# Norms and operand splits made piece by piece inside the projections, and squares summed beside the residual update

## The chip, the cores and the metric

The kernel runs on one core of a Trainium2 chip. The metric is the device time of one execution in microseconds (us); less is better. The engines are TensorE (PE in the profile, with its weight loads as PEld), VectorE (DVE), ScalarE (ACT), GpSimd (POOL) and SyncE (SP), which here only issues transfers. PEclk is the granted clock of TensorE as a share of its full 2.4 GHz; 0.50 is the lower level of 1.2 GHz.

## The reference

Two transformer blocks on 1024 tokens of width 1024. The first has two layers with 256 context tokens (1280 columns in all): a layer of attention and a layer of gated linear attention (GLA). The second has 16 meta tokens in front (1040 columns), three mixers, gates and a mixture of experts. What matters here is this frame, which comes three times, and the two residual updates between:

```
def rms_norm(x, g):
    y = x * lax.rsqrt(jnp.mean(x * x, axis=-1, keepdims=True) + EPS)
    return y * g
...
for layer in range(2):
    hx = rms_norm(x, norm_g[layer]) * (1.0 + scx) + shx
    hc = rms_norm(ctx, norm_g[layer]) * (1.0 + scc) + shc
    ox, oc = mixer(hx @ w_in, hc @ w_in)
    x = x + gtx * (ox @ w_out[layer])
    ctx = ctx + gtc * (oc @ w_out[layer])
...
u = rms_norm(concat(meta, x), norm1_g)
p = u @ w_in
...
merged = g0 * ya + g1 * yb + g2 * (fox @ w_out_c)
h = h + merged @ w_o
```

The modulation (shift, scale, gate) of layer 0 comes from `silu(c) @ adaln_w[0]`, made at the very start.

## The kernel before

Activations lie transposed: 128 partitions of features by columns of tokens, in 8 chunks `k` of 128 features. The residual `E.X` stays in SBUF. A projection is computed with three products per weight and operand block: each fp32 operand is split in a rounded high part (`hi`, made by ACT) and a rest (`lo`, made by DVE as operand minus `hi`), and TensorE adds `w_hi*hi + w_hi*lo + w_lo*hi`. A **job** is one block of 128 output features: 8 chunks x 3 products x its column tiles, accumulated in one of two PSUM tiles `acc`. Tiles are `TILES1` (512, 512, 256 columns), `XT` (512, 512), `TILES2` (352, 352, 336) or `TILES3` (512, 512). ACT makes `w_hi` (L616) and DVE `w_lo` (L730) of job i+2 when job i is done; weights are loaded by SP in a ring of three.

The program is a chain of phases, each a block that every engine enters together and leaves together. Six phases only prepare operands for the projection that follows, and the projection starts when the whole phase is over:

1. `setup_phase`: loads parameters, then the weights of the first modulation (8 transfers of 1536 KB, half on SP, half on ACT). TensorE multiplies them (L289). GpSimd loads the residual (L243, 5120 KB) once the second of them has landed.
2. `norm_phase`, three times (before the layer-0, the GLA and the second block's projection): ACT squares each chunk (L330), TensorE sums over partitions with a matrix of ones (L369), ACT takes `rstd` with Ln and Exp (L336, L338), DVE makes `u = x * gain * rstd` (L397), ACT makes `hi` (L354, L352), DVE makes `lo` (L385, L383). SP loads the first two weights (L448), which are split by one ACT and one DVE instruction of 2048 columns (L452, L456) after the second tile.
3. `split_phase`, three times (before the two output projections and the gate projection): SP loads pieces of the mixer's result (L982) in a ring, ACT makes `hi` (L993), DVE `lo` (L1000), then the first two weights. Before the second output projection SP also restores the residual from DRAM (L986), and the phase waits for it.

Within `gemm_phase` a job goes over all its tiles for each chunk and product, the loop that the change takes apart:

```
for k in range(nk):
    kb = (j.k0 + k) * P
    for lhs, rhs in ((whi, hi), (whi, lo), (wlo, hi)):
        first, last = k == 0 and lhs is whi and rhs is hi, k == nk - 1 and lhs is wlo
        for t, (off, n) in enumerate(j.tiles):
            mmi = eng.matmul(a[:, t, 0:n], lhs[:, j.w % 2, kb:kb + P],
```

A job's result leaves PSUM by kind: "store" by ACT (L673), "rope" (L687, L688, `roots`, and DVE) with small products on TensorE in the next job (`rope_aux`), "resid" by DVE into `E.X` (L847), "gate" by DVE (L882 to L890). Job i+2 waits until job i has left its PSUM tile.

## Time and profile before

| what | value |
|---|---|
| time, median of 3 runs | 3600.99 us (3600.76 to 3604.33) |
| profiled execution, its own time | 3605.53 us |
| its span | 3603.7 us |
| PE busy | 2956.3 us (82%) |
| DVE busy | 1624.4 us (45%) |
| ACT busy | 1231.2 us (34%) |
| DMA | 452.02 MB, 125 GB/s over the span |

Busy shares are means over phases that differ much. What a preparation phase costs is read from the stretch between the last work of the phase ahead of it and the first product of the projection.

### The profile page before, as it was taken

The numbers are of one execution on the slowest core, as the hardware profiler recorded it, in microseconds if no ns is written. First come the engines' busy times: TensorE is split into PE (matmuls) and PEld (weight loads), VectorE is DVE, ScalarE is ACT, GpSimd is POOL, SyncE is SP. The second block draws the span as 40 slices with busy tenths as digits, with TensorE's granted clock in tenths as the row PEclk, the third lists the DMA queues.
The fourth block names the chain that finished last, engine by engine and source line by source line (L and its number), as shares of the span: only waits on it lengthen the run. The fifth ranks groups of instructions, "written<-read, shape, count | busy, mean of one in ns | idle before, by whom it ended". The sixth has DMA issues, their size and how long they took to land. (4 is left out here: it accounts for less than half of the span.)

```text
span 3603.7 us, 36460 instructions
## 1 busy us (share of the span) xinstructions
PE 2956.3 (82%) x14078; PEld 2306.6 (64%) x14078; DVE 1624.4 (45%) x2616; ACT 1231.2 (34%) x1972; POOL 159.5 (4%) x258
## 2 busy tenths in 40 slices
PE   7799997957775979996894889999897378748883
PEld 2577885636664758883663679988665267637773
DVE  1566335637774130005553235431243453357786
ACT  2444212435553131113432221111143211237776
POOL 0000000100000000000000000000000020020002
PEclk9899998979997979996897989999999699769997
DMA  5223333253303013221214013333332641269996
GB/s 221 88 105 134 135 122 87 72 155 98 81 8 107 18 53 132 85 70 66 79 36 165 23 60 122 114 102 97 95 97 54 251 133 59 90 238 357 371 384 253
DMA packets 144304, 452.02 MB, mean 125 GB/s; under 512 B 18258, under 2 KB 39378, under 8 KB 142836
## 3 DMA queue, kind: packets, MB, share of 16 engines
q1 hardware_dynamic: 100196, 280.78, 23.1%
q0 software_dynamic: 27520, 98.02, 7.9%
q10 hardware_dynamic: 16416, 70.90, 5.4%
q8 instruction: 112, 1.84, 0.2%
q14 instruction: 60, 0.49, 0.0%
HBM read 322.68 MB, written 126.95 MB: 125 GB/s over the span
## 5 line engine op out<-in xcount | busy, mean ns | idle before, releaser
L948 PE MATMUL acc<-act_hi,w_hi 128*128 128x512 f32 (+3 forms) x2512 | 704.5, 378 | 204.0 <-PEq L967 110.2
L948 PE MATMUL acc<-act_lo,w_hi 128*128 128x512 f32 (+3 forms) x2512 | 685.2, 370 | 0.0
L948 PE MATMUL acc<-act_hi,w_lo 128*128 128x512 f32 (+3 forms) x2512 | 683.5, 370 | 0.0
L948 PEld LDWEIGHTS acc<-act_hi,w_hi 128*128 128x128 f32 x2512 | 449.8, 191 | 300.3 <-issue 220.8
L730 DVE TENSOR_TENSOR w_lo<-w_stage,w_hi 128x1024 fp32r<-128x1024 f32 x114 | 139.7, 1225 | 921.8 <-ACT w_hi L616 921.8
L948 PEld LDWEIGHTS acc<-act_lo,w_hi 128*128 128x128 f32 x2512 | 447.1, 191 | 80.2
L948 PEld LDWEIGHTS acc<-act_hi,w_lo 128*128 128x128 f32 x2512 | 445.5, 190 | 78.7
L616 ACT ACTIVATE w_hi<-w_stage 128x1024 fp32r<-128x1024 f32 x114 | 120.9, 1060 | 1073.2 <-PE acc L948 1073.2
L2670 DVE TENSOR_TENSOR expert_lo<-expert_stage,expert_hi 128x1024 fp32r<-128x1024 f32 x186 | 225.9, 1223 | 80.6 <-ACT expert_hi L2613 78.1
L2613 ACT ACTIVATE expert_hi<-expert_stage 128x1024 fp32r<-128x1024 f32 x186 | 195.8, 1058 | 91.7 <-DMA expert_stage<-in_exp_w 46.4
L1722 DVE TENSOR_REDUCE max<-scores 128x1 f32<-128x256 f32 (+6 forms) x256 | 117.2, 484 | 148.9 <-PE scores L1846 148.0
L1886 PE MATMUL outputs<-probs_t,v_ones 128*128 128x512 f32 (+2 forms) x392 | 172.2, 520 | 2.2 <-ACT probs_t L1677 2.2
L1677 ACT ACTIVATE probs_t<-scores_t 128x512 f32<-128x512 f32 (+4 forms) x196 | 100.6, 514 | 135.6 <-PE scores_t L1872 132.9
L1265 DVE TENSOR_REDUCE stats<-scores 128x1 f32<-128x1280 f32 (+1 forms) x80 | 102.0, 1275 | 70.6 <-PE scores L1419 70.4
L1864 PE MATMUL scores_t<-q_stack,k_hi 128*128 128x512 f32 (+4 forms) x196 | 122.8, 627 | 2.5 <-ACT q_rows L1694 2.5
L1221 ACT ACTIVATE probs<-scores,stats 128x1280 f32<-128x1280 f32 (+1 forms) x80 | 92.2, 1153 | 64.3 <-DVE stats L1271 64.1
L1414 PE MATMUL scores<-k_hi,q_stack 128*128 128x512 f32 (+1 forms) x208 | 88.5, 426 | 30.4 <-DMA k_lo<-rope 29.3
L2835 PE MATMUL expert_up<-expert_hi,slots_hi 128*128 128x512 f32 x248 | 101.8, 410 | 6.4 <-DVE slots_lo L2675 6.4
L673 ACT ACTIVATE out_stage<-acc 128x512 f32<-128x512 f32 (+1 forms) x168 | 80.3, 541 | 64.7 <-PE acc L948 64.7
L1842 PE MATMUL scores<-k_hi,q_stack 128*128 128x256 f32 (+6 forms) x256 | 94.8, 373 | 7.2 <-DVE max L1722 5.7
L2837 PE MATMUL expert_up<-expert_hi,slots_lo 128*128 128x512 f32 x248 | 98.8, 398 | 0.0
L2836 PE MATMUL expert_up<-expert_lo,slots_hi 128*128 128x512 f32 x248 | 98.7, 398 | 0.0
(360 smaller groups left out, 4236.8 us busy)
## 6 DMA issues: line engine op xcount, KB each, us to landing
expert_stage<-in_exp_w SPq DMA_DIRECT2D x186, 512.0 KB, 6.5
w_stage<-in_w_in SPq DMA_DIRECT2D x43, 512.0 KB, 4.3
rope<-out_stage ACTq DMA_DIRECT2D x26, 640.0 KB, 3.6
proj<-out_stage ACTq DMA_DIRECT2D x26, 640.0 KB, 5.3
slots_in<-zero SPq DMA_DIRECT2D x1, 15872.0 KB, 42.3
residual<-slots_in POOLq DMA_DIRECT2D x31, 512.0 KB, 7.3
slots_out<-residual POOLq DMA_DIRECT2D x31, 512.0 KB, 6.7
w_stage<-in_ab_w_in SPq DMA_DIRECT2D x26, 512.0 KB, 5.0
```

The source lines that it names most:

```text
L616: eng.activation(whi[:, w % 2, :], stage[:, w % NSTG, :], ACT.Copy).then_inc(w_hi, 1)
L730: eng.tensor_tensor(wlo[:, w % 2, :], stage[:, w % NSTG, :], whi[:, w % 2, :].bitcast(F32), ALU.subtract).then_inc(w_lo, 1)
L948: mmi = eng.matmul(a[:, t, 0:n], lhs[:, j.w % 2, kb:kb + P], rhs[:, c0 + k, off:off + n], start=first, stop=last)
L1265: chain(eng.tensor_reduce(st[:, q % 4, 0:1], S[s_of[q]][:, 0:u.width], AX, ALU.max))
L1677: eng.activation(pT[0:w, q % 3, c0:512], ST[q % 2][0:w, c0:512], ACT.Exp, scale=SCALE).then_inc(exped, 1)
L1722: eng.tensor_reduce(mx[:, n % 2, h, pc:pc + 1], SP[p % 3][:, 0:k1 - k0], AX, ALU.max).then_inc(max_done, 1)
L1864: eng.matmul(s[:, c0:512], kh[:, c, tok:tok + P], qs[:, n % QS, c0:512], start=True, stop=False)
L1886: eng.matmul(O[n % 2][:, c0:512], v1[0:w, u.pair % VS, u.side, tok // P, :], pT[0:w, q % 3, c0:512], start=fox and b == 0, stop=b == len(u ...
L2613: eng.activation(whi[:, n % R, :], stage[:, n % NS, :], ACT.Copy).then_inc(w_hi, 1)
L2670: eng.tensor_tensor(wlo[:, n % R, :], stage[:, n % NS, :], whi[:, n % R, :].bitcast(F32), ALU.subtract).then_inc(w_lo, 1)
L2835: eng.matmul(UP[j % 2][:], uh, wh, start=k == 0, stop=False)
L2837: mm = eng.matmul(UP[j % 2][:], ul, wh, start=False, stop=k == KD - 1)
```

## The change

`norm_phase` and `split_phase` are gone. `gemm_phase` takes a `Feed`: a list of operand pieces (tile, chunk) that ACT and DVE make inside the projection's own block, ahead of their work on jobs, with the two weights split one by one in between. TensorE waits for each piece by number. The first `lead` = 2 jobs are run tile by tile: tile 0 of job 0, tile 0 of job 1, tile 1 of job 0, and so on; from job 2 on all is as before. In the gate projection `lead` is 0. The columns' square sums come from a running tile `E.sums`, kept in `setup_phase` for the first norm and in the two output projections (ACT squares each updated residual chunk, DVE adds it) for the others; one product per tile with the matrix of ones remains. In `setup_phase` the residual is loaded ahead of the modulation's weights, on SP and ACT. The restore of the residual before the second output projection moves to GpSimd, inside the block. In the layer-0 projection the second job is now a "store" job.

```diff
 setup_phase
@@ sync (scalar the same with odd i)
-            eng.wait_ge(loaded, 48)
+            for i in range(0, KD, 2):
+                eng.dma_start(E.X[:, i, X0:X0 + NT1], dram["x0"][:, i, :]).then_inc(x_in[i], 16)
+                eng.dma_start(E.X[:, i, 0:META], dram["meta"][:, i, :]).then_inc(x_in[i], 16)
             for i in range(0, KD, 2):
                 eng.dma_start(tiles[:, i, :], dram["adaln_w0"][i]).then_inc(w_in[i], 16)
@@ scalar
+            for i in range(KD):
+                eng.wait_ge(x_in[i], 32)
+                if i >= 3:
+                    eng.wait_ge(summed, i - 2)
+                eng.activation(E.sums[:] if i == 0 else sq[:, i % 2, :], E.X[:, i, :], ACT.Square).then_inc(sq_ready, 1)
 gemm_phase
@@ sync
+            if feed.src is not None:
+                load_operand(0)
+            for w in range(NW):
+                if w >= NSTG:
+                    eng.wait_ge(w_lo, w - NSTG + 1)
                 eng.dma_start(stage[:, w % NSTG, :], wdram[w]).then_inc(w_in[w % NSTG], 16)
+                if w == 1 and feed.src is not None:
+                    for i in range(1, len(feed.pieces)):
+                        load_operand(i)
@@ gpsimd
+            if restore is not None:
+                for i in range(KD // 2):
+                    eng.dma_start(E.X[:, 2 * i:2 * i + 2, 0:META + T], restore[:, 2 * i:2 * i + 2, :]).then_inc(restored[i], 16)
@@ scalar
+            if feed.norm is not None:
+                mean_root(0)
+            round_w(0)
+            for i, (t, k, _, _) in enumerate(feed.pieces):
+                operand_high(i)
+                if i == 1:
+                    round_w(1)
+                if feed.norm is not None and k == 5 and t + 1 < len(feed.tiles):
+                    mean_root(t + 1)
             for i, j in enumerate(jobs):
+                if sums and i >= 1:
+                    squares(i - 1)
@@ vector
+            if feed.norm is not None:
+                normalized(0)
+                normalized(1)
+            split_w(0)
+            for i in range(len(feed.pieces)):
+                operand_low(i)
+                if feed.norm is not None and i + 2 < len(feed.pieces):
+                    normalized(i + 2)
+                if i == 1:
+                    split_w(1)
+            eng.wait_ge(fed_lo, len(feed.pieces))
@@ tensor
+            for t in range(len(jobs[0].tiles) if lead else 0):
+                for i in range(lead):
+                    if t == 0:
+                        eng.wait_ge(w_lo, jobs[i].w + 1)
+                    products(i, [t])
@@ in products, ahead of each product
+                            if hi is feed.hi and feed.number.get((c0 + k, off), 0) > fed[0]:
+                                fed[0] = feed.number[c0 + k, off]
+                                eng.wait_ge(fed_lo, fed[0])
```

On TensorE, from the setup to the first projection, stood before (the `acc` rows are job 0):

```order
L289 MATMUL mod_rows_p<-adaln_w,silu_cond 2x512 x48
L294 MATMUL mod<-consts,mod_rows 128x2 x24
L215 UNCONDITIONAL_BRANCH
L363 UNCONDITIONAL_BRANCH
L369 MATMUL ss_31<-sq,consts 128x512 x8
L369 MATMUL ss_32<-sq,consts 128x512 x8
L369 MATMUL ss_33<-sq,consts 128x256 x8
L303 UNCONDITIONAL_BRANCH
L913 UNCONDITIONAL_BRANCH
L948 MATMUL acc_43<-act_hi,w_hi 128x512 x2
L948 MATMUL acc_43<-act_hi,w_hi 128x256
```

and stands now, at the same place (`acc_40` is the PSUM tile of job 1, used for the sums first):

```order
L307 MATMUL mod<-consts,mod_rows 128x2 x23
L216 UNCONDITIONAL_BRANCH
L907 UNCONDITIONAL_BRANCH [waits barrier_Pool_Activation_PE_DVE_SP_release]
L950 MATMUL acc_40<-square_sums,consts 128x512 x2
L950 MATMUL acc_40<-square_sums,consts 128x256
L941 MATMUL acc_39<-act_hi,w_hi 128x512 [waits operand_lo_ready_54,w_lo_ready_45]
L941 MATMUL acc_39<-act_lo,w_hi 128x512
L941 MATMUL acc_39<-act_hi,w_lo 128x512
L941 MATMUL acc_39<-act_hi,w_hi 128x512 [waits operand_lo_ready_54]
L941 MATMUL acc_39<-act_lo,w_hi 128x512
```

24 products of the norm became 3, the phase border between norm and projection is gone, and the projection's first products wait for single pieces.

On ACT, in the layer-0 projection, stood before (`acc_44` is job 1; the first row is the last of the roots of job 0, which wait for small products that TensorE makes inside job 1):

```order
L633 ACTIVATE out_stage<-rope_x 128x256 [waits rope_done_70]
L626 DMA rope<-out_stage 128x1280 [waits out_lo_ready_58]
L626 DMA rope<-out_stage 128x1280
L616 ACTIVATE w_hi<-w_stage 128x1024 [waits w_loaded0_45,products_50]
L687 ACTIVATE rope_sq<-acc_44 128x512 [waits products_50,out_lo_ready_58]
```

and stands now (`acc_40` is job 1):

```order
L561 ACTIVATE out_stage<-rope_x 128x512 [waits rope_done_72]
L561 ACTIVATE out_stage<-rope_x 128x256 [waits rope_done_72]
L554 DMA rope<-out_stage 128x1280 [waits out_lo_ready_60]
L554 DMA rope<-out_stage 128x1280
L544 ACTIVATE w_hi<-w_stage 128x1024 [waits w_loaded0_41,products_46]
L647 ACTIVATE out_stage<-acc_40 128x512 [waits products_46] x2
```

The order is the same, but the small products of job 0 now stand inside job 2, so the split of the fourth weight, which job 3 needs, waits for job 2 where it waited for job 1.

On SP, in the second output projection, stood before (with a phase border ahead of the last row):

```order
L982 DMA stage<-mixed 128x512 x6
L448 DMA w_stage<-in_w_out 128x1024 x2
L982 DMA stage<-mixed 128x512 x10
L986 DMA residual<-residual_x 128x8x1040
L571 DMA w_stage<-in_w_out 128x1024 x6
```

and stands now (the pieces' tiles are named `operand`, six of them in turn):

```order
L486 DMA operand_331<-mixed 128x512
L493 DMA w_stage<-in_w_out 128x1024 x2
L486 DMA operand_332<-mixed 128x512
L486 DMA operand_333<-mixed 128x512
L486 DMA operand_334<-mixed 128x512
L486 DMA operand_335<-mixed 128x512
L486 DMA operand_336<-mixed 128x512
```

The first weights stand behind one piece and no longer behind six, and the restore is on GpSimd's queue.

## Rows read from the trace of the kernel before

**Rows 1.** Busy time by stretch: start:end, length, PE, PEld, DVE, ACT, POOL, PEclk, DMA, GB/s

```profile
64.70:117.40 52.70, 24.48 (x49) 10.39 (x49) 30.45 (x49) 33.81 (x57) 0.00 (x0) 0.66 0.06 20
...
1109.90:1134.90 25.00, 0.00 (x0) 0.01 (x1) 15.38 (x17) 13.59 (x17) 0.00 (x0) 0.50 0.70 252
...
1251.90:1304.90 53.00, 26.31 (x48) 10.94 (x49) 30.45 (x49) 33.76 (x56) 0.00 (x0) 0.64 0.05 20
...
1923.60:1954.00 30.40, 0.00 (x0) 0.00 (x0) 13.11 (x17) 11.87 (x17) 0.00 (x0) 0.50 0.86 313
...
2045.40:2087.40 42.00, 18.48 (x49) 10.39 (x49) 25.00 (x49) 27.95 (x57) 0.00 (x0) 0.74 0.07 25
...
2845.90:2865.50 19.60, 0.02 (x1) 0.05 (x1) 7.69 (x9) 6.81 (x9) 0.00 (x0) 0.50 0.50 161
```

**Rows 2.** The same view around the first norm and the first projection's start

```profile
64.70:81.70 17.00, 15.01 (x29) 6.56 (x30) 0.00 (x0) 12.21 (x19) 0.00 (x0) 0.79 0.19 62
...
117.40:122.80 5.40, 5.40 (x15) 4.43 (x16) 0.00 (x0) 1.22 (x1) 0.56 (x1) 0.50 0.80 297
122.80:150.00 27.20, 27.20 (x131) 21.71 (x130) 7.46 (x11) 9.97 (x16) 0.00 (x0) 0.99 0.24 96
```

**Rows 3.** ACT in order of time: the splits of the third and later weights

```profile
152.21 1.06 ACT L616 ACTIVATE w_hi<-w_stage 128x1024 fp32r<-128x1024 f32 x1 [1.62 <-PE acc L948]
...
1165.76 1.06 ACT L616 ACTIVATE w_hi<-w_stage 128x1024 fp32r<-128x1024 f32 x1 [13.02 <-PE acc L948]
1179.84 1.06 ACT L616 ACTIVATE w_hi<-w_stage 128x1024 fp32r<-128x1024 f32 x1 [13.02 <-PE acc L948]
...
1329.77 1.06 ACT L616 ACTIVATE w_hi<-w_stage 128x1024 fp32r<-128x1024 f32 x1 [8.85 <-PE acc L948]
...
1340.65 1.06 ACT L616 ACTIVATE w_hi<-w_stage 128x1024 fp32r<-128x1024 f32 x1 [8.85 <-PE acc L948]
...
1978.63 1.06 ACT L616 ACTIVATE w_hi<-w_stage 128x1024 fp32r<-128x1024 f32 x1 [9.82 <-PE acc L948]
...
2101.42 1.06 ACT L616 ACTIVATE w_hi<-w_stage 128x1024 fp32r<-128x1024 f32 x1 [12.81 <-PE acc L948]
...
2112.84 1.06 ACT L616 ACTIVATE w_hi<-w_stage 128x1024 fp32r<-128x1024 f32 x1 [5.75 <-PE acc L948]
```

**Rows 4.** DVE in order of time: two pieces running in the first and third norm

```profile
85.95 0.75 DVE L397 SCALAR_TENSOR_TENSOR u<-residual,mod_gain,rstd 128x512 f32<-128x512 f32 x1
...
87.28 0.75 DVE L397 SCALAR_TENSOR_TENSOR u<-residual,mod_gain,rstd 128x512 f32<-128x512 f32 x1
...
2061.56 0.58 DVE L397 SCALAR_TENSOR_TENSOR u<-residual,params,rstd 128x352 f32<-128x352 f32 x1
...
2062.49 0.58 DVE L397 SCALAR_TENSOR_TENSOR u<-residual,params,rstd 128x352 f32<-128x352 f32 x1
```

**Rows 5.** Tile view of the operand's rest: ns min/median/max, first and last start

```profile
L385 DVE SCALAR_TENSOR_TENSOR act_lo<-u,mod,act_hi x48: 475/746/753, 85.3 to 1304.1; 128x512 fp32r<-128x512 f32 x32, 128x256 fp32r<-128x256 f32 x16
```

**Rows 6.** The page's costliest groups: the weights' rests

```profile
L730 DVE TENSOR_TENSOR w_lo<-w_stage,w_hi 128x1024 fp32r<-128x1024 f32 x114 | 139.7, 1225 | 921.8 <-ACT w_hi L616 921.8
```

**Rows 7.** Issue to landing: the first norm's two weights (L448), then the restore (L986)

```profile
DMA to landing us min/median/max: 3.6/4.0/4.5
...
DMA to landing us min/median/max: 15.6/15.6/15.6
```

**Rows 8.** Busy time by stretch, inside the first split phase

```profile
1118.00:1121.00 3.00, 0.00 (x0) 0.00 (x0) 1.75 (x3) 0.85 (x2) 0.00 (x0) 0.50 1.02 412
```

**Rows 9.** The setup: TensorE in order of time, and the residual's load

```profile
15.18 44.08 PE L289 MATMUL mod_rows_p<-adaln_w,silu_cond 128*2 128x512 f32 x96 [15.18 <-DMA adaln_w<-in_adaln_w]
...
residual<-in_x POOLq DMA_DIRECT2D x1, 5120.0 KB, 33.9
```

**Rows 10.** The gate projection: first way out of PSUM, and the third weight

```profile
2871.04 1.42 DVE L882 TENSOR_TENSOR residual<-acc,gates 128x512 f32<-128x512 f32 x2 [5.86 <-PE acc L948]
...
2879.32 1.06 ACT L616 ACTIVATE w_hi<-w_stage 128x1024 fp32r<-128x1024 f32 x1 [16.46 <-PE acc L948]
```

More of the change, by code:

```diff
@@ L837, in _ @@
                     split_w(j.w + 2)
+                if sums and i >= 1:
+                    add_squares(i - 1)
                 a = acc[i % 2]
-                if j.kind == "he":
-                    hidden(i, j)
-                    continue
+                if restore is not None and i % 2 == 0:
+                    eng.wait_ge(restored[i // 2], 16)
                 for t, (off, n) in enumerate(j.tiles):
@@ L951, in _ @@
                                 mmi.then_inc(mm, 1)
-                    if k % 2 == 1 and pending:
+                    if i >= lead and k % 2 == 1 and pending:
                         rope_aux(*pending.pop(0))
-                while pending:
-                    rope_aux(*pending.pop(0))
+            if feed.norm is not None:
+                for t, (off, n) in enumerate(feed.tiles):
+                    eng.matmul(acc[1][:, t, 0:n], col(E.con, CONST_AT, "ones"), feed.norm.sums_of(off, n),
+                               start=True, stop=True).then_inc(ss_done, 1)
@@ new lines, in _ @@
+            for t in range(len(jobs[0].tiles) if lead else 0):
[3 more added lines that the diff above has]
+                    products(i, [t])
+            for i, j in enumerate(jobs):
+                if i >= lead:
+                    eng.wait_ge(w_lo, j.w + 1)
+                    if i >= 2:
+                        eng.wait_ge(free[i % 2], free_before[i])
+                    if j.a.merged:
+                        eng.wait_ge(m_lo, 2 * KD)
+                    products(i, range(len(j.tiles)))
+                    while pending:
+                        rope_aux(*pending.pop(0))
@@ L2924, in out_proj @@
                         gate_of=lambda t, f=f: E.mod[:, layer, 32 + 2 * f + (t == 2):32 + 2 * f + (t == 2) + 1])
-                    for f in range(KD)])
+                    for f in range(KD)], feed, restore=restore, sums=True)
         par = lambda name, j=None: col(E.par, PARAM_AT, name, j)
@@ L2955, in qblocks @@
             return [(P * b, P) for b in bl] + ctxb, masks
+        first.close()
         def head(r, a):
@@ L3006, in build @@
             wts = Weights(nc, c, [d["w_in"][f] for f in order])
-            norm_phase(nc, E, lambda k, off, n: E.X[:, k, off:off + n], TILES2, lambda k, t: par("norm1", k),
-                       lambda k, t: None, hi, lo, wts=wts)
+            norm = Norm(lambda k, off, n: E.X[:, k, off:off + n], lambda off, n: E.sums[:, off:off + n],
+                        lambda k, t: par("norm1", k), lambda k, t: None)
+            feed = Feed([(t, k, *tile) for t, tile in enumerate(TILES2) for k in range(KD)], hi, lo, 2, 4, norm=norm, tiles=TILES2)
             jobs = []
```

433 lines of the change are left out of this document (175 added, 258 removed).

## The prediction

> **What bounds the kernel now.** I read the stretches between phases first, since the change removes phase borders. The busy view shows six stretches in which the projection's products stand still while operands are made [rows 1]: 52.7, 25.0, 53.0, 30.4, 42.0 and 19.6 us, 222.7 us together, 6% of the span. In the three split stretches TensorE does nothing; in the norms it only sums squares. Next I read what fills a stretch. The first norm spends 17.0 us before the first `rstd` exists [rows 2], then DVE paces it: a new 512-column piece starts every 1.33 us (85.95 to 87.28) and a 352-column one every 0.93 us [rows 4]. Third, the jobs: ACT splits a weight when a job ends, so the starts of these splits date the jobs. A job takes 14.08 us with three tiles, 10.88 us with two, 11.42 us with 1040 columns [rows 3]. Last the clock: after each stretch the granted clock is 0.50 for about 5.4 us, 15 products, and 0.99 behind [rows 2], so each projection pays some 2.5 us at its start.
>
> **The yardstick.** For each projection I compare the moment at which job 2 can start, counted from the start S of the preparation. Before, it is the end of job 1, read from the splits [rows 3] and the starts of the stretches [rows 1]: 152.2 - 64.7 = 87.5, 1165.8 - 1109.9 = 55.9, 1329.8 - 1251.9 = 77.9, 1978.6 - 1923.6 = 55.0, 2112.8 - 2045.4 = 67.4 us. From job 2 on the programs are the same.
>
> **First and second norm.** The sums are ready when the block starts, so squares and 21 of 24 fp32 products are gone from the path, and three are left beside the load of the first weight, which lands 3.6 us after issue [rows 7]. Then ACT rounds it, 1.06 us [rows 3], DVE splits it, 1.23 us [rows 6], and the first piece's rest takes 0.75 us [rows 5]; with hand-overs the first product starts at S+7.2. Pieces follow at 1.33 us [rows 4], and the second weight's split puts 1.1 us in: piece 15 at 7.2 + 1.1 + 15 x 1.33 = 28.3, and the 8 pieces of 256 columns at some 0.8 us (two operations of 0.475 us [rows 5], less the overlap) at S+34.7. TensorE needs 3 products a piece and job, 0.68 us at full clock (10.88 / 16 pieces [rows 3]). So tile 0 of job 0 follows DVE to S+18.3, tile 0 of job 1 takes 5.4, tile 1 of both ends at S+35, and in the first norm tile 2 of both, 2.7 us each, at S+40.7. ACT is late next: it is done with pieces at 34.5, and at the end of job 0 (S+38) rounds the third weight and takes job 0 out of PSUM, some 4.4 us: job 2 starts at S+42.5. Its rope work adds what it added to job 1 before, 152.2 - 64.7 - 52.7 - 2 x 14.08 - 2.5 = 4.1 us. And the fourth weight's split now stands behind roots that need job 2. Before, the roots and stores ended with job 1; rounding and split behind them, 1.06 + 1.23 us, now hold job 3, while DVE and the stores ahead do no more than before: 2.5 us, unless another job covers it. First norm: 87.5 - (42.5 + 4.1 + 2.5) = 38.4. In the GLA projection the leading jobs have two tiles, but ACT and DVE first finish the context pieces (S+34.7), then the third weight (2.3 us more with hand-over): job 2 at S+37, gain 77.9 - 37 = 40.9. I take 38 and 41.
>
> **Third norm.** Pieces of 0.93 us [rows 4]: the first at S+6.9, the last at 6.9 + 1.1 + 23 x 0.92 = S+29.2. Job 1's last tile behind it is a third of 11.42: S+33.5. Gain 67.4 - 33.5 = 33.9; I take 33.5.
>
> **First output projection.** The first weight now stands behind one piece and no longer behind six, so the first product comes at S+7.6. At 412 GB/s [rows 8] a 256 KB piece takes 0.64 us; with six slots, 4.0 us to a landing [rows 7] and two splits behind it, 0.8. That is near TensorE's own 0.68, which therefore sets the end: 7.6 + 2.5 (low clock) + 28.2 = S+38.3, and the third weight's split and DVE's way out make it S+39. Gain 55.9 - 39 = 17. The third weight's load is issued behind all 23 pieces, about S+22, and needed at S+35, so it is covered. **Second output projection.** GpSimd issues the restore at once. It took 15.6 us alone [rows 7]; beside the pieces both halve the rate, and the first product comes at S+9.3. Sixteen pieces at 1.3 us last to S+27, TensorE needs until 9.3 + 2.5 + 2 x 10.88 = S+33.6, or 35.7 where it waits. Gain 55.0 - 35.7 = 19. Before, the phase waited for this restore; now DVE wants its first quarter only at S+33.
>
> **What is added.** ACT's squares and DVE's additions run inside jobs that last 10.9 or 14.1 us and cost nothing, but not behind the last job: DVE adds 2 or 3 tiles at 0.7 us (1.42 us for two [rows 10]), 3.2 us for both projections. **Gate projection.** Its first two jobs need no pieces and start at S+7, but DVE takes nothing out of PSUM until all 16 pieces are split, at 0.8 us each about S+17, where it did so at 2871.0 - 2845.9 = S+25.2; the third weight was rounded at S+33.4 [rows 10]. Gain 7, bounds 3 and 9.
>
> **Setup.** Here the change costs. TensorE works without a break from 15.2 to 59.3 [rows 9], fed by the first weight, and the residual came after. Now 5120 KB of residual on two queues stand ahead. By the shapes SP moves 0.98 MB of parameters, 2.65 MB of residual and 1.57 MB of weight until then; at half of 412 GB/s [rows 8] that is 25 us, and with 2 us to the first byte TensorE starts at 27: 12 us lost, with nothing to cover it. Bounds: 0, if SP's queue had the whole rate; 15, if the 1024 short rows of meta tokens cost extra. I take 12, as both queues are full from the start. The residual itself took 33.9 us behind the weights [rows 9], which shows that a queue's place decides. The Trainium skill ("DMA: Bandwidth & Descriptors", section "Issuing engines are not separate DMA queues") says that transfers of all issuers run on the same 16 engines and interleave. By that rule the residual delays the weights by its bytes whoever issues it, 12 to 13 us, as in my sum.
>
> **Sum.** 38 + 17 + 41 + 19 + 33.5 + 7 - 3.2 - 12 = 140.3. TensorE is only half busy while it follows the pieces, so some time at low clock is likely behind them: I take off 1 us for each of five projections. 135 us less of the profiled execution's 3605.5, which lies 4.5 above the median of the runs shown; from the median 3601 it gives 3466.
>
> **Rivals.**
> *The low clock stays through both leading jobs* (0.07). While it waits for pieces, TensorE at half clock needs all of the 1.33 us (2 x 0.68), at full clock half. For it: the norm stretches, with TensorE busy 24.5 of 52.7 us, show 0.66, and the following work starts at 0.50 [rows 1, 2]. Against: that busy time is scattered, while at the low level the pieces keep it full, as in the 5.4 us that raised the clock [rows 2]. Price: leading jobs at twice the time, ends at S+59, 59, 48, 50 and 48: 80 us in all; of 140 remain 60, 3541. [...]
> *A piece goes hand to hand* (0.05): `u`, `hi`, `lo` one after the other, 0.75 + 0.72 + 0.75 = 2.2 us in place of 1.33. Against: [rows 4] already show the overlap with one piece ahead, and now two are. Price 19 + 19 + 16 us, 3520.
> *Slower* (0.02): the low clock outlasts the leading jobs. A three-tile job would take 28 and not 14 us. With the first rival's 80 us, 60 are left, so five such jobs decide it; two more in each of five projections, 12 us each in the mean, give 3601 - 60 + 120 = 3661. Against: in [rows 2] the clock rises within 5.4 us of full work.
> *It doesn't do what it says* (0.03): the setup loses 15 and early starts end in ACT's late ways out, each projection half of its gain: 155.5 / 2 - 3.2 - 15 = 60, 3541.
>
> **How the numbers follow.** My forecast has 0.83. Its own range is 3445 to 3495: setup without loss and gate at 9 (-14), clock kept (-5), against setup at 15, 2 to 5 us more in each of five projections. The range to hold it 8 in 10 reaches toward the rivals, all on one side: 3442 to 3510. A measurement tells 0.2%, 7 us: faster 0.97, same 0.01 (a part of the last rival), slower 0.02.
>
> **What would show it.** The first L302 product of the setup at about 27 us and its end at 71; the first L941 product 7 to 9 us after each block starts; job 2 at S+42, 39, 37, 36, 34; granted clock over 0.9 across the leading jobs behind the first 8 pieces; L782 every 1.33 us; the restore landing without a wait. Wrong would be a clock of 0.5 to the end of job 1, pieces over 2 us apart, or a setup that ends at 60.

## The result, and the profile after

The changed kernel takes 3482.49 us (median of four runs), the kernel before 3600.88 us in the same comparison. One of the four (4906.55 us, mean granted clock 0.566) was disturbed: it is left out of the ratio, but not of this median, and the other three have 3475.6, 3478.8 and 3486.17. The ratio is 0.9664, with a 95% interval of 0.9643 to 0.9685, or 121 us less (113 to 129). The forecast was 3466, 135 less. The profiled execution took 3478.8 us with a span of 3476.9, 126.8 less than the span of before.

I cut the span at the first transfer that SP issues in each block, in order of time:

```profile
84.22 0.81 SPq L493 DMA_DIRECT2D w_stage<-in_ab_w_in  x2
...
1087.82 0.32 SPq L486 DMA_DIRECT2D operand<-mixed  x1
...
1214.24 0.80 SPq L493 DMA_DIRECT2D w_stage<-in_gla_w_in  x2
...
1843.65 0.32 SPq L486 DMA_DIRECT2D operand<-mixed  x1
...
1953.14 1.28 SPq L493 DMA_DIRECT2D w_stage<-in_w_in  x3
...
2720.75 0.32 SPq L486 DMA_DIRECT2D residual<-fox  x1
```

Against the starts in [rows 1] this gives the length of each part. The forecast column has the terms of the prediction's sum, the tail of the square sums halved between the output projections:

| from the start of ... to the next | before | after | difference | forecast |
|---|---|---|---|---|
| setup | 64.7 | 84.2 | +19.5 | +12 |
| layer-0 projection, attention | 1045.2 | 1003.6 | -41.6 | -38 |
| first output projection | 142.0 | 126.4 | -15.6 | -15.4 |
| GLA projection and layer | 671.7 | 629.4 | -42.3 | -41 |
| second output projection | 121.8 | 109.5 | -12.3 | -17.4 |
| third norm's projection to branches | 800.5 | 767.6 | -32.9 | -33.5 |
| gate projection to the end | 757.8 | 756.2 | -1.6 | -7 |
| low clock, allowed for | | | | +5 |
| sum | | | -126.8 | -135 |

**Setup.** TensorE in order of time, then the two queues until 37 us and, below, from 10 to 20 us (packets, MB, share of the 16 engines' time; q1 is SP's, q10 ACT's):

```profile
36.73 42.85 PE L302 MATMUL mod_rows_p<-adaln_w,silu_cond 128*2 128x512 f32 x96 [36.73 <-DMA adaln_w<-in_adaln_w]
```

```profile
q10 hardware_dynamic: 1707, 8.88, 58.8%
q1 hardware_dynamic: 1753, 5.51, 38.4%
...
DMA packets 1406, 4.17 MB, mean 417 GB/s; under 512 B 769, under 2 KB 769, under 8 KB 1285
...
q10 hardware_dynamic: 703, 2.74, 67.9%
q1 hardware_dynamic: 703, 1.43, 36.8%
```

The first product comes 21.5 us later than in [rows 9], and since it waits for SP's first weight, SP's share decides. From 10 to 20 us the packets of both queues are equally many (703 and 703), their bytes are not: ACT's are twice as large. The Trainium skill ("DMA: Bandwidth & Descriptors", section "Queues, rings and completion order") says that each DMA engine alternates between queues packet by packet. The trace agrees. It has a packet for each row, and 769 of the 1406 are under 512 B: most of these are the 64-byte rows of the meta tokens, each of which takes a turn of its queue. By the sizes of the packets in the trace they are 346 of SP's 703 packets in these 10 us, and 121 of ACT's 703 are already rows of weights, 12 KB each. From 5 to 10 us, with SP's queue on parameters and long rows and ACT's with 240 of the 64-byte rows, the packets were equal again (438 and 428), and SP's queue had the larger part of the bytes, 1.30 MB against 0.74.

**Leading jobs.** Busy time by stretch, columns as in [rows 1]: the layer-0 projection to job 2, the second output projection (in two stretches), the third norm's projection (in two), the gate projection to job 2:

```profile
84.20:91.10 6.90, 4.04 (x7) 1.76 (x7) 3.38 (x5) 5.83 (x7) 0.00 (x0) 0.75 0.86 320
91.10:110.00 18.90, 16.22 (x59) 11.12 (x60) 18.90 (x29) 11.18 (x17) 0.00 (x0) 0.91 0.23 78
110.00:125.60 15.60, 14.51 (x87) 12.83 (x85) 9.02 (x20) 8.63 (x16) 0.70 (x1) 1.00 0.22 71
1851.40:1869.20 17.80, 14.23 (x28) 8.11 (x29) 8.97 (x13) 8.51 (x13) 0.00 (x0) 0.50 1.00 385
1869.20:1884.80 15.60, 15.60 (x69) 12.89 (x69) 4.94 (x7) 4.23 (x6) 0.00 (x0) 1.00 0.44 155
1959.50:1970.00 10.50, 9.70 (x35) 8.33 (x36) 10.44 (x22) 5.79 (x12) 0.00 (x0) 0.58 0.33 101
1970.00:1986.00 16.00, 16.00 (x103) 16.00 (x102) 12.63 (x27) 8.89 (x19) 0.00 (x0) 1.00 0.00 1
2720.20:2742.00 21.80, 8.44 (x25) 6.42 (x25) 10.23 (x21) 8.23 (x18) 1.67 (x3) 0.66 0.69 213
```

In the norms DVE is the full column while pieces run; the clock is up after a few us in the layer-0 projection and within 10.5 us in the third. In the layer-0 and the GLA projection it rose behind six products back to back, and then stayed at 1.00 through groups of three products every 1.33 us. In the second output projection the clock stays at 0.50 for 17.8 us, with the wires full (385 GB/s). In the gate projection TensorE is busy 8.4 of 21.8 us. Pieces in the first norm's projection, DVE in order of time, answer to [rows 4]: 1.33 us apart.

```profile
101.34 0.75 DVE L782 SCALAR_TENSOR_TENSOR rope_t<-residual,mod_gain,square_sums 128x512 f32<-128x512 f32 x1
102.67 0.75 DVE L782 SCALAR_TENSOR_TENSOR rope_sq<-residual,mod_gain,square_sums 128x512 f32<-128x512 f32 x1
```

TensorE in order of time, where jobs 2 and 3 start in the layer-0 projection, and job 2 in the first output, the GLA, the second output, the third norm's and the gate projection:

```profile
125.64 0.70 PE L941 MATMUL acc<-act_hi,w_hi 128*128 128x512 f32 x2 [1.13 <-ACT rope_x L664]
...
146.19 0.70 PE L941 MATMUL acc<-act_hi,w_hi 128*128 128x512 f32 x2 [2.43 <-DVE w_lo L696]
...
1126.23 0.70 PE L941 MATMUL acc<-act_hi,w_hi 128*128 128x512 f32 x2 [1.40 <-DVE residual L840]
...
1249.83 0.50 PE L941 MATMUL acc<-act_hi,w_hi 128*128 128x512 f32 x1 [1.00 <-DVE w_lo L696]
...
1884.82 0.61 PE L941 MATMUL acc<-act_hi,w_hi 128*128 128x512 f32 x2
...
1987.32 0.64 PE L941 MATMUL acc<-act_hi,w_hi 128*128 128x352 f32 x3
...
2741.95 1.19 PE L941 MATMUL acc<-act_hi,w_hi 128*128 128x512 f32 x2 [6.33 <-issue]
```

Minus the starts, job 2 of the first five: 41.4, 38.4, 35.6, 41.2 and 34.2 us (forecast 42.5, 39, 37, 35.7 and 33.5); job 3 of the first waits 2.43 us (forecast 2.5). On the page, the idle time ahead of the products' first group fell from 204.0 us, most of it at phase borders, to 119.1:

```profile
L941 PE MATMUL acc<-act_hi,w_hi 128*128 128x512 f32 (+3 forms) x2512 | 730.3, 380 | 119.1 <-DVE act_lo L792 44.6
```

### The profile page after: what moved, and what is told of

Same layout as the page of the kernel before. It is cut to its first block and busy times, and to the rows that moved or that the text cites. A ratio compares the mean times of both kernels' runs of the same rounds, so it can differ in the third digit from the quotient of the medians.

```text
span 3476.9 us, 36313 instructions
## 1 busy us (share of the span) xinstructions
PE 2904.1 (84%) x13952; PEld 2276.5 (65%) x13952; DVE 1655.2 (48%) x2683; ACT 1230.1 (35%) x1968; POOL 161.0 (5%) x260
## 3 DMA queue, kind: packets, MB, share of 16 engines
q1 hardware_dynamic: 102612, 279.18, 23.9%
## 5 line engine op out<-in xcount | busy, mean ns | idle before, releaser
L941 PE MATMUL acc<-act_hi,w_hi 128*128 128x512 f32 (+3 forms) x2512 | 730.3, 380 | 119.1 <-DVE act_lo L792 44.6
L941 PE MATMUL acc<-act_lo,w_hi 128*128 128x512 f32 (+3 forms) x2512 | 707.9, 371 | 0.0
L941 PE MATMUL acc<-act_hi,w_lo 128*128 128x512 f32 (+3 forms) x2512 | 706.5, 370 | 0.0
L696 DVE TENSOR_TENSOR w_lo<-w_stage,w_hi 128x1024 fp32r<-128x1024 f32 x126 | 154.3, 1225 | 828.6 <-ACT w_hi L544 828.6
L544 ACT ACTIVATE w_hi<-w_stage 128x1024 fp32r<-128x1024 f32 x126 | 133.3, 1058 | 957.6 <-PE acc L941 919.8
L1645 ACT ACTIVATE probs_t<-scores_t 128x512 f32<-128x512 f32 (+4 forms) x196 | 100.7, 515 | 135.6 <-PE scores_t L1840 132.8
L647 ACT ACTIVATE out_stage<-acc 128x512 f32<-128x512 f32 (+1 forms) x168 | 80.3, 542 | 64.7 <-PE acc L941 64.7
## 6 DMA issues: line engine op xcount, KB each, us to landing
slots_in<-zero SPq DMA_DIRECT2D x1, 15872.0 KB, 42.5
```

The lines of the kernel that those rows point to most:

```text
L544: eng.activation(whi[:, w % 2, :], stage[:, w % NSTG, :], ACT.Copy).then_inc(w_hi, 1)
L696: eng.tensor_tensor(wlo[:, w % 2, :], stage[:, w % NSTG, :], whi[:, w % 2, :].bitcast(F32), ALU.subtract).then_inc(w_lo, 1)
L941: mmi = eng.matmul(a[:, t, 0:n], lhs[:, j.w % 2, kb:kb + P], rhs[:, c0 + k, off:off + n], start=first, stop=last)
L1645: eng.activation(pT[0:w, q % 3, c0:512], ST[q % 2][0:w, c0:512], ACT.Exp, scale=SCALE).then_inc(exped, 1)
```

## The experiments

All these kernels are edits of the changed kernel. Differences to it are those of the ratios, times 3600 us; each ratio is known to about 0.2%, so a difference to some 10 us, and where an edit is worth less its block is read from the trace. For that, each kernel's blocks come from one profiled execution. "S" is the start of the block, as above.

| kernel | ratio to before | 95% interval | to the changed kernel |
|---|---|---|---|
| changed kernel | 0.9664 | 0.9643 to 0.9685 | |
| e1_x_behind | 0.9623 | 0.9600 to 0.9646 | -15 |
| e2_odd_first | 0.9632 | 0.9612 to 0.9651 | -12 |
| e3_pieces_first | 0.9937 | 0.9917 to 0.9957 | +98 |
| e4_restore_later | 0.9651 | 0.9630 to 0.9673 | -5 |
| e5_squares_on_path | 0.9818 | 0.9787 to 0.9849 | +55 |
| e6_gate_out_earlier | 0.9656 | 0.9626 to 0.9685 | -3 |
| e7_first_squares_only | 0.9640 | 0.9620 to 0.9660 | -9 |
| e8_all | 0.9571 | 0.9547 to 0.9595 | -33 |
| e9_queues_held | 0.9662 | 0.9635 to 0.9689 | -1 |
| e11_exp_first | 0.9611 | 0.9593 to 0.9629 | -19 |
| e12_all_exp_first | 0.9557 | 0.9540 to 0.9574 | -39 |
| e13_best | 0.9549 | 0.9530 to 0.9569 | -41 |

### What the overlap is worth

```diff
 gemm_phase, tensor
+            if lead:
+                eng.wait_ge(fed_lo, len(feed.pieces))
             for t in range(len(jobs[0].tiles) if lead else 0):
```

> The changed kernel, but in the five projections whose first two jobs run tile by tile, TensorE's first product waits until all operand pieces are split. Theory (the gain of the change is mainly that the two leading jobs run beside the pieces): pieces end at 33, 26, 34, 26 and 29 us after the block starts; then 2.5 us at the low clock and 28.2, 28.2, 21.8, 21.8 and 22.8 us of products, against a start of job 2 at 41.4, 38.4, 35.6, 41.3 and 33.4 now: 23, 19, 24, 10 and 22 us more, 98 in all, 3577. Rival (the gain comes from the squares and from the phase borders that are gone, the overlap is worth little because TensorE at the low clock or in groups of three products is slow): at most 40 us more.

Measured 98 us more. The five blocks grew by 25.4, 18.8, 21.3, 13.8 and 18.4 us, 97.7 together. The rival (at most 40 us) falls: running the two leading jobs beside the pieces is the larger part of the gain.

### What the squares are worth

```diff
 gemm_phase, scalar, ahead of mean_root(0)
+                for q, (t, k) in enumerate(sq_pieces):
+                    ...
+                    eng.activation(slots[q % 4][:, 0:n], feed.norm.x_of(k, off, n), ACT.Square).then_inc(nsq, 1)
+                eng.wait_ge(nsq_used, len(sq_pieces))
 gemm_phase, tensor: 24 sums of these squares in place of the 3 products
```

> The changed kernel, but the three norms take their squares again at the start of the block: ACT squares 24 chunks into the four operand slots, TensorE sums each with the matrix of ones, and the first root follows all 24. The squares beside the residual update stay as they are. Theory (moving the squares off the path is worth the time of these 24 steps): the three stretches from the block's start to the first product grow from 6.9, 6.9 and 6.3 us to 24, 24 and 20.5; ACT's square of 512 columns and TensorE's fp32 sum take 0.85 us a step, 0.6 for 352 columns; 17 + 17 + 14 = 48 us more than the changed kernel, less up to 2.5 us for each of the three starts, if the sums lift TensorE's clock for the products behind them: 3522 to 3530. Rival (ACT squares while DVE and the loads are busy with the first weight anyway, so only the part beyond the load counts): under 35 us more.

Measured 55 us more, by the ratios; the squares beside the residual update stay, so this is the price of the second set on the path. The first product came at S+26.7, 25.7 and 23.2, that is 19.8, 18.8 and 16.9 us later, 55.5 together. More than my 48: TensorE's sums set the pace, and it began them at the low clock, as its rows in order of time show. A sum is two instructions, so a row holds two sums: 3.78 us at first, 1.88 later.

```profile
86.94 3.78 PE L959 MATMUL acc<-rope_t,consts 128*128 128x512 f32 x4 [3.13 <-ACT rope_t L623]
...
92.94 1.88 PE L959 MATMUL acc<-rope_t,consts 128*128 128x512 f32 x4
```

The rival, under 35, falls.

### What the squares cost where they went

In this kernel the squares of 7 of the 8 chunks are left out in both output projections, so that the norms behind them scale by incomplete sums.

```diff
 gemm_phase, scalar
-                if sums and i >= 1:
+                if sums and i == 1:
                     squares(i - 1)
 squares(NJ - 1) behind the last job left out
 gemm_phase, vector: all add_squares left out
```

> The changed kernel with the squares left out in both output projections for all chunks but the first, so 7 of 8 ACT squares and all of DVE's additions there are gone (the sums are then incomplete, and the norms behind them scale wrongly). Theory (inside the jobs they are hidden, only the last job's tail counts): the blocks of the two output projections, 126.4 and 109.5 us long in the changed kernel, lose 2.5 to 3.3 and 1.8 to 2.5 us at their end and nothing before, 5 us in all, 3477. Rival (ACT's squares delay the split of the next weight, and DVE's additions the way out of PSUM, in each job): 0.5 us in each of 16 jobs more, 10 to 13 us in all.

The ratios differ by 9 us with an uncertainty of 10, which settles nothing, so I read the blocks: 124.9 and 108.2 us. The same blocks in the kernels that don't edit them take 126.9 and 109.6 in the mean (126.0 to 127.7 and 108.7 to 110.3), so the squares cost 2.0 and 1.4, 3.4 together, less than the 5 of my theory. Most of it stands at the end of the block, where TensorE waits for the next one. At the end of the first output projection, in the changed kernel and in this one:

```profile
1214.29 1.19 PE L950 MATMUL acc<-square_sums,consts 128*128 128x512 f32 x1 [3.34 <-PEq L362]
...
1217.07 0.67 PE L944 MATMUL acc<-square_sums,consts 128*128 128x512 f32 x1 [1.81 <-PEq L362]
```

The wait is 1.5 us shorter, and 1.4 at the end of the second (2.93 against 1.54), 2.9 together. The rest, 0.5 us, is within the spread of the blocks: the squares are hidden in the jobs, only the tail counts (3.2 in the prediction), and the rival's 10 to 13 us fall.

### Setup: the order of the loads

```diff
 e1_x_behind: setup_phase, sync; scalar the same with odd i
             for i in range(0, KD, 2):
                 eng.dma_start(tiles[:, i, :], dram["adaln_w0"][i]).then_inc(w_in[i], 16)
+            for i in range(0, KD, 2):
+                eng.dma_start(E.X[:, i, X0:X0 + NT1], dram["x0"][:, i, :]).then_inc(x_in[i], 16)
+                ...
 e2_odd_first: setup_phase, tensor
-            for i in range(KD):
+            for n, i in enumerate([1, 3, 5, 7, 0, 2, 4, 6]):
```

> The changed kernel, but in the setup each of SP's and ACT's queue holds its four modulation weights first and its chunks of the residual behind them. My theory (the residual's 5 MB ahead of the weights cost 19.5 us, because the first weight stands behind them on SP's queue): the first product of the setup at about 15 us and the last at 59, the squares done by 56 beside them, the next block starts at 65, 19.5 us less than the changed kernel, 3459. Rival 1 (the order only moves the wait: the squares now come last): the residual lands at 48 to 50 us, four ACT squares and DVE additions of 1.3 and 1.5 us stand behind it and the block starts at 70 or later, 14 us less at most. Rival 2 (the late start comes from the many small transfers or from the queues themselves, not from the bytes ahead): the first product stays near 30 us and the gain is under 8.

> The changed kernel with its transfers as they are, but TensorE takes the four weights of ACT's queue (1, 3, 5, 7) first and those of SP's queue (0, 2, 4, 6) behind them. Theory (the two queues do not share the rate equally: in the changed kernel ACT's queue moved 8.9 MB in the first 37 us and SP's 5.5, and the first weight needed is on the slower one): ACT's weights landed at 22.3, 26.4, 33.2 and 40.5 us there, a weight takes 5.5 us of TensorE, so the setup's products start at 22 and end at 22 + 44 + at most 2 of waits = 68, and the block starts at 73, 11 us less, 3468. Rival (it is the bytes ahead on both queues alike, 27 us at equal shares): the start moves to 27 at best and the gain stays under 9. Rival 2: nothing moves, since TensorE waits for the end of all transfers at 48 us: 0.

In e1_x_behind the first product came at 23.80 us and the block started at 73.2: 11 us less, and not the 19.5 I expected. None of the three stories fits. The block's start is within rival 1, but not for its reason: the sums ended at 56 us and the products at 67.7. The first product is not near 30, as rival 2 has it, though the short rows moved behind the weights with all the rest, so that this run does not clear them. What it waited for was SP's first weight: until 24 us SP's queue moved 593 packets with 2.76 MB, ACT's, full of weights, 557 with 6.25 MB.

In e2_odd_first the first product came at 22.85 and the block started at 71.6, 12.7 us less, against 11 forecast; its rivals (under 9, and 0) fall. With the same bytes in the same order, ACT's first weight lands 14 us ahead of SP's. Of these, some 5 us are an estimate for the 0.98 MB of parameters that only SP's queue has in front, at half of 412 GB/s. ACT's weight alone would also fit equal shares (4.2 MB at half of 412 GB/s are 20.5 us); that the shares are unequal is shown by the counts of packets and bytes above.

The next kernel also holds ACT's queue until the parameters are in, as before the change:

```diff
 e9_queues_held: setup_phase, sync and scalar
+            eng.wait_ge(loaded, 48)
             (the four weights, then the residual)
```

> The changed kernel with the modulation's weights ahead of the residual, as in e1_x_behind, and besides both queues wait for the parameters, constants and masks before they issue the first weight, as in the kernel before. Theory (in e1_x_behind the first weight landed only at 23.8 us, because ACT's queue filled the wires from 0.8 us on, while SP's first weight stood behind the small loads; holding ACT back gives it to SP): first product at 15 us, last at 59, the next block starts at 65 if the squares of the last chunks, whose loads end near 55, are done by 59, which is 20 us less than the changed kernel. Rival (the first weight at 15 us in the kernel before came from the residual not being queued at all; with it queued behind, its transfers mix with the weights): start at 15 but TensorE waits for later weights, end at 64 or more. Rival 2 (the squares are last): the block starts at 68 or later, with ACT and DVE ending after TensorE.

The block started at 81.2 us, almost as late as in the changed kernel; all three stories are wrong (the first product came at 33, and the sums ended at 55.4, long before the products). ACT's own rows of e9_queues_held in order of time say why ("q" marks the issue of a transfer):

```profile
9.89 0.53 ACTq L251 DMA_DIRECT2D residual<-in_x  x1
10.45 8.61 ACTq L252 DMA_DIRECT2D residual<-in_meta  x1
19.09 6.38 ACTq L251 DMA_DIRECT2D residual<-in_x  x1
25.49 6.42 ACTq L252 DMA_DIRECT2D residual<-in_meta  x1
31.95 0.21 ACT L254 ACTIVATE sigma_cond<-params 128x16 f32<-128x16 f32 x1 [29.92 <-issue]
...
33.01 43.55 PE L304 MATMUL mod_rows_p<-adaln_w,silu_cond 128*2 128x512 f32 x96 [33.01 <-DVE silu_cond L272]
```

From its tenth transfer on, ACT stands 6 to 9 us in each issue (in the changed kernel, where the residual goes first, all twelve were issued by 7.4 us), and the small exponential, which TensorE's condition needs, stands behind them in the program. A new theory, and its test, is to move only the exponentials:

```diff
 e11_exp_first, to e9_queues_held: setup_phase, scalar
+            eng.activation(sg[:], col(E.par, PARAM_AT, "cond"), ACT.Exp, scale=-1.0).then_inc(asteps, 1)
+            ...
             (ACT's residual transfers)
-            eng.activation(sg[:], ...
```

> e9_queues_held with one edit: ACT runs the two exponentials of the setup (the condition's and lambda's) ahead of its eight residual issues, which in e9_queues_held stood ahead of them. Theory (there the first weight had landed, but TensorE waited until 33.0 us for the condition, because ACT stood in its DMA issues, 8.6, 6.4 and 6.4 us each, until earlier transfers made room): first product of the setup at 15 to 16 us, its last ends at 60, the next block starts at 65, against 81.2 in e9_queues_held and 84.2 in the changed kernel: 16 and 19 us less. Rival (the issues were slow because the engines of the transfers were full, and the first weights are slow for the same reason): first product at 20 us or later. Rival 2 (the squares now end last, since ACT's residual issues start later): the block starts at 70 or later.

```profile
15.11 44.02 PE L304 MATMUL mod_rows_p<-adaln_w,silu_cond 128*2 128x512 f32 x96 [15.11 <-DMA adaln_w<-in_adaln_w]
```

The block starts at 64.5 us, 16.7 less than in e9_queues_held and 19.7 less than in the changed kernel, where the kernel before had 64.7. Squares and sums end at 55.3, beside the products. So the squares are free in the setup; the order of the transfers, and of ACT's work among them, made the whole loss.

### Second output projection: the restore

```diff
 gemm_phase, gpsimd
             if restore is not None:
+                eng.wait_ge(fed_lo, 12)
                 for i in range(KD // 2):
```

> The changed kernel, but in the second output projection GpSimd issues the restore of the residual only when 12 of the 16 pieces are split. Theory (the restore's 4.3 MB share the rate with the pieces, which makes the pieces' pace 2 us instead of 0.8): pieces at 0.7 to 0.9 us apart behind the first, job 2 starts at 33 us after the block's start instead of 41.3, the first quarter of the restore lands before 33, so 8 us less, 3471. Rival (the pieces' pace is set by the six slots and the time to a landing, the restore is not it): under 2 us less. Rival 2 (the wait moves to the restore's end): DVE waits for the first quarter, and no gain.

By the ratios 5 us less; the block is 100.3 us long instead of 109.5, 9.2 less, and job 2 starts at S+32.0 instead of S+41.2. Between the first product and job 2, by stretch:

```profile
1854.70:1860.00 5.30, 5.27 (x12) 3.80 (x13) 5.01 (x8) 4.17 (x7) 0.00 (x0) 0.50 0.84 291
1860.00:1879.60 19.60, 19.60 (x87) 16.19 (x86) 8.46 (x12) 7.38 (x11) 2.81 (x4) 0.99 1.00 369
```

TensorE has its pieces, works without a gap, and the clock rises after 5.3 us, as in [rows 2], instead of 17.8. The run doesn't part the two, what the pieces' pace costs and what the clock costs. In the changed kernel the queues moved, from 1852 to 1864 us (q0 is GpSimd's, columns as above):

```profile
q0 software_dynamic: 849, 3.30, 68.0%
q1 hardware_dynamic: 867, 1.58, 34.7%
```

Again as many packets, and twice the bytes for the other queue. Both rivals fall.

### Gate projection: the way out of job 0

```diff
 gemm_phase, vector, in the loop over the pieces
+                if i == 6 and not lead:
+                    out_of(0)
```

> The changed kernel, but in the gate projection DVE takes job 0 out of PSUM behind the seventh of the 16 operand pieces, and no longer behind the last. Theory (the changed kernel gained only 1.8 us in this block, where 7 were expected, because job 2 waits until DVE has split all pieces, 20.2 us after the start, and TensorE stood still for 6.3 us): job 0 leaves PSUM at 14 us, job 2 follows the pieces and ends 6 us earlier; the third weight is rounded at 23 us after the block's start instead of 29, and the gain reaches the end of the block in so far as the gates' loads keep up: 4 to 6 us. Rival 1 (pieces come at the pace of their loads, 1.2 us each with four slots, and job 2 waits for the last piece anyway): 3 us or less, since the last piece stays at 20. Rival 2 (what is gained is lost again to the gates' loads within ten jobs): the third weight earlier, the end of the block not.

The third weight is rounded at S+23.9 instead of S+29.1: rival 1 falls. But the block's last weight is rounded at S+217.3 (216.2 to 217.3 in the four kernels with this edit), where the nine without it have 216.3 to 224.0. Rival 2 holds in its outcome, not in its cause, for this kernel. A group of three jobs takes 16.0 us in one kernel and 17.0 in another. The same group in e6_gate_out_earlier and in e9_queues_held, by TensorE's wait and by stretch:

```profile
2822.49 1.19 PE L948 MATMUL acc<-act_hi,w_hi 128*128 128x512 f32 x2 [3.03 <-DVE gated L865]
...
2816.70:2833.75 17.05, 14.02 (x49) 10.90 (x48) 9.25 (x13) 2.32 (x3) 3.22 (x6) 0.80 0.41 126
```

```profile
2813.80 0.71 PE L943 MATMUL acc<-act_hi,w_hi 128*128 128x512 f32 x2 [3.03 <-DVE gated L882]
...
2808.00:2823.80 15.80, 11.66 (x49) 8.88 (x49) 9.26 (x13) 2.35 (x4) 3.23 (x6) 1.00 0.47 136
```

The same 3.03 us wait, and the first pair of products behind it takes 1.19 us at half clock or 0.71 at full. Of the seven groups behind the third weight's, the kernel before had one of 17.0 us, the changed kernel three, e6_gate_out_earlier four, e9_queues_held none. All four kernels with the edit have four or five such groups, of the nine without it six have none, the others two, three and five. With five on both sides, e12_all_exp_first (with the edit) has its last weight at S+217.0 and e11_exp_first, whose gate projection differs only by the edit, at S+224.0. So at the same clock the edit was worth 7 us, and against kernels without slow groups the clock took it back. Why the clock falls in one kernel and not in the other, and whether the edit makes it fall, stays open.

### All together

```diff
 e8_all = restore_later + gate_out_earlier + weights ahead of the residual, even ones on ACT's queue, taken 0, 2, 1, 4, 3, 6, 5, 7
 and in the layer-0 projection, scalar:
-                if i >= 1 and jobs[i - 1].kind == "rope":
-                    roots(i - 1)
+                late = lead and jobs[0].kind == "rope"
+                if late and i == 2:
+                    roots(0)
 (DVE: split_w(3) ahead of job 0's rope work)
 e12_all_exp_first = e8_all + exponentials ahead of the residual's transfers
 e13_best = e8_all with the setup of e11_exp_first in place of its own
```

> Four edits together on the changed kernel. (1) Setup: weights ahead of the residual, the even ones on ACT's queue, which has nothing in front of them, and TensorE takes them in the order 0, 2, 1, 4, 3, 6, 5, 7: start at 10 to 11 us (the activation of the condition is ready at 9.8), end at 55, next block at 60, 24 us less. (2) GpSimd's restore issued behind the twelfth piece, 9 us less. (3) In the gate projection job 0 leaves PSUM behind the seventh piece, 4 to 6 us less. (4) In the layer-0 projection the fourth weight is split, and job 1 taken out, ahead of the roots of job 0: job 3 starts without the 2.4 us wait. Sum 40: 3440. Rival for (1): the two queues' shares differ again, a weight of SP's queue is late by 5 to 10 us, and the block starts at 65 to 70. Rival for (4): the wait moves to the roots of job 0, which hold job 2's way out and thereby job 4, no gain.

> e8_all with the same edit. There the weights lay on the swapped queues and the condition came at 20.3 us, for the same reason. Theory: the first product follows the parameters and the condition's small steps, 10 to 12 us, and as TensorE needs 5.5 us for a weight it works without a break of more than 2 us, end at 56, next block at 60 to 62, against 68.6 in e8_all: 7 to 8 us less, 3438. Rival (the parameters share the rate with ACT's weights, so they land later than 8 us, and TensorE starts at 14 to 16): block at 64 to 66, 3 to 4 us less. The clock of TensorE in the gate projection can add or take 5 us, whatever the setup does.

> The setup of e11_exp_first (both queues held until the parameters landed, weights ahead of the residual, exponentials ahead of ACT's residual issues) with the other three edits of e8_all (restore behind the twelfth piece, job 0 of the gate projection out earlier, job 1 and the fourth weight ahead of the roots in the layer-0 projection). Theory: the edits lie in different blocks and add up: first block at 64.5 us as in e11_exp_first, 19.7 less than the changed kernel, layer-0 projection and attention 3.6 to 4 less, second output projection 9 less, gate projection 5 less at its third weight, of which 0 to 5 arrive, as TensorE's clock falls or not in its 3 us waits: 33 to 38 us less than the changed kernel, 3437 to 3442. Rival (an earlier start in one block is paid in a later one): less than 25.

e8_all: 3445.57 us. Its first block started at 68.6 and not at 60, because here too ACT's exponential (19.26 us) stood behind issues. The fourth weight is rounded at S+41.0 instead of S+59.5, job 3 no longer waits, and the layer-0 block, attention included, is 999.8 us long, and 1000.9 and 1001.7 in the next two kernels, where the kernels without this edit have 1003.0 to 1006.6: 3 to 5 us less than their mean, and its rival falls.

e12_all_exp_first: 3439.59 us, first block at 67.0. The rival holds, and by more than it said (first product at 17.6 us): the parameters landed only at 16.5 us. On the ACT row the wait names its last transfer:

```profile
16.50 0.22 ACT L249 ACTIVATE sigma_cond<-params 128x16 f32<-128x16 f32 x1 [14.47 <-DMA mask<-in_masks]
```

Until 16 us SP's queue moved 442 packets with 1.10 MB, ACT's 409 with 4.63 MB. Small rows beside large ones got 19% of the bytes.

e13_best: 3433.30 us (3427.39 to 3441.43), ratio 0.9549, 41 us less than the changed kernel where 33 to 38 were expected. First block at 64.5, second output projection 100.7 us long. It beats the kernel before and the changed kernel; from e12_all_exp_first (0.9557) the ratios don't tell it apart.

## Why the prediction was right, and where its terms were off

**Direction and size.** The forecast was 135 us less; the profile shows 126.8 and the ratio 121, whose interval of 113 to 129 doesn't reach the forecast, but lies within its range. Of the 16.5 us between 3466 and 3482.49, 8 are this difference, 4.5 are that the profiled execution of before lay above its median, and 3.7 come from the disturbed run, which is counted in the median of the changed kernel. The misses in the setup, the second output projection and the gate projection (7.5, 5.1 and 5.4 us) are partly made up by the norms and by the allowance for the clock.

**The norms.** Terms 38, 41 and 33.5; measured 41.6, 42.3 and 32.9. The steps hold one by one: first product at S+6.9, 6.9 and 6.3, pieces at 1.33 us, job 2 at S+41.4, S+35.6 and S+34.2, job 3's wait 2.43 us. e3_pieces_first and e5_squares_on_path show that both halves of the mechanism carry it. Undone alone, the overlap costs 98 us in the five projections and the squares' place 55 in the three norms.

**First output projection.** 15.6 against 15.4, with job 2 at S+38.4.

**Second output projection.** The term "both halve the rate", 19, was mis-sized: 13.7 before the tail of 1.4. The restore did not take half but 68% of the wires' time and two thirds of the bytes; pieces came 2.0 us apart instead of 1.3, and TensorE's clock stayed low for 17.8 us. Here, and only here, my first rival happened, and in part: the clock rose at 1869.2, behind 4 us of products without a wait, and the rest of the leading jobs ran at 1.00. The Trainium skill ("TensorE: Matmul & The Clock Gate", section "HAM oscillation") tells of groups of some 2 us of products between waits of 3 to 5 us, and of each group starting at half clock. The waits here were shorter, 1.74 us once and up to 0.5 us then, so this is another case, and no run shows by itself why the clock stayed low. e4_restore_later gives 9.2 us back.

**Setup.** The term 12 was mis-sized, measured 19.5, outside its bounds of 0 to 15. The step that failed is "at half of 412 GB/s": SP's queue moved its 5.2 MB until the first weight in 34.7 us, 150 GB/s and not 206, because the queues took turns by packet. ACT's queue, with no parameters in front, came to the weights and their 12 KB packets earlier, and 512 of the packets ahead of SP's first weight were 64-byte rows of meta tokens. My bound of 15 had named these rows; no run moves them alone, so how the 7.5 us divide between the two stays open. That the residual cost time at all was right, and, in this order, that it had "nothing to cover it". e11_exp_first shows that it was avoidable.

**Gate projection.** The term 7 with bounds 3 to 9; the profile shows 1.6. By the third weight it was 4.3 (S+29.1 against S+33.4): pieces ended at S+19.7 and not at S+17, since ACT waited for their loads six times, 6.3 us together. Later groups of three jobs lost 2 us to the clock in this execution. The rest of the block varies on its own (below).

**Low clock.** 5 us were allowed, one for each projection. In four of the five the clock rose within 3 to 9 us of the first product, and of these blocks only the third norm's was longer than forecast, by 0.6 us.

**Tail of the squares.** 3.2 forecast, 2.9 measured at the borders, 3.4 by the length of the blocks.

## What to carry to other kernels

A preparation phase in front of a matrix product is worth taking apart into pieces when an engine other than TensorE sets its pace: running the first two jobs tile by tile beside it hid 98 of 3600 us here. What is loaded earlier "because it is needed anyway" has to be priced by what then stands behind it, on the wires and in the issuing engine's program: a transfer of large rows on another queue took more than its half here, and compute behind many issues waited for the wires. Let the small loads that everything needs land first, hold the others back until then, and keep an engine's small critical work ahead of its long list of issues.

## What the runs showed of the hardware that was not expected

- Two busy queues share by packets and not by bytes: 703 and 703 packets but 2.74 and 1.43 MB in 10 us, 849 and 867 packets but 3.30 and 1.58 MB in 12 us, 409 and 442 packets but 4.63 and 1.10 MB in 16 us. A packet was one row here: a 64-byte row takes a turn as a 12 KB row does.
- An engine that issued large transfers first stopped in later issues. In e9_queues_held, with four weights in front, the first nine of ACT's took 0.5 us each, the later ones 8.61, 6.38 and 6.42 us. In the changed kernel, with the weights last, none of ACT's twelve took over 0.9.
- The same wait of 3.03 us in the same group of jobs ended at half clock in one kernel and at full clock in another, worth about 1 us each time.
- From the last weight of the gate projection to the end, twelve profiled kernels that are the same there took 528.8 to 541.1 us. Single times of a kernel spread by up to 20 us, so an edit worth less than 10 us is read from its own block.
